# A two-layer decoder step on one core: attention groups regrouped, the last weight chunk cut by tokens, and four waits of the blocks split or reordered

## The reference

```python
for i in range(2):
    x = x + 0.5 * swiglu(rmsnorm(x, ...), w_in, w_out)      # ffn1, inner width 2816
    h = rmsnorm(x, ...)
    y = s5_mixer(h, ...) if i == 0 else hgrn2_mixer(h, ...) # diagonal SSM / gated linear recurrence, 8 heads
    x = x + y
    x = x + cross_attend(rmsnorm(x, ...), mem_k[i], mem_v[i], w_q, w_o)  # 4 heads of 256, 256 memory tokens
    x = x + 0.5 * swiglu(rmsnorm(x, ...), w_in, w_out)      # ffn2
x = rmsnorm(x, final_norm)
```

## Time and profile before

| | us |
|---|---|
| median of 3 runs (lowest, highest) | 2386.51 (2385.75, 2387.01) |
| the profiled execution, its whole time | 2385.19 |
| its span, first to last instruction | 2383.4 |
| PE busy in it | 2351.9 |
| DVE busy | 1291.9 |
| ACT busy | 872.1 |
| POOL busy | 605.3 |

### The profile page before, as it was taken

One profiled execution on the slowest core, in us unless ns is written; L12 is line 12 of the kernel. 1 busy time (PEld: TensorE's weight loads), 2 busy tenths in 40 slices (PEclk: granted clock), 3 DMA queues, 4 the chain that ended last, 5 costly groups with the idle time before them and its releaser, 6 DMA issues.

```text
span 2383.4 us, 50169 instructions
## 1 busy us (share of the span) xinstructions
PE 2351.9 (99%) x21068; PEld 2289.6 (96%) x21068; DVE 1291.9 (54%) x1903; ACT 872.1 (37%) x1398; POOL 605.3 (25%) x591
## 2 busy tenths in 40 slices
PE   8999999999999999999999999999999999999999
PEld 8999999889979999999999999999998969999998
DVE  6654643964575543446543344577777666443442
ACT  4422333543233331232333233267774233221322
POOL 3779957431103000004111010442122103000003
PEclk9999999999999999999999999999999999999999
DMA  5456445563563333333543333333332653333332
GB/s 161 131 156 152 118 122 162 178 177 106 152 237 93 95 95 91 98 103 94 160 116 110 104 104 111 91 99 101 101 108 75 211 186 89 97 93 93 97 101 85
DMA packets 483707, 289.19 MB, mean 121 GB/s; under 512 B 22289, under 2 KB 466962, under 8 KB 482514
## 3 DMA queue, kind: packets, MB, share of 16 engines
q1 hardware_dynamic: 477856, 280.66, 39.8%
q0 software_dynamic: 560, 1.84, 0.6%
q10 hardware_dynamic: 5122, 4.25, 0.5%
HBM read 258.86 MB, written 27.85 MB: 120 GB/s over the span
## 4 chain that ended last, share of the span: by engine, by line
PE 90%; POOL 3%; DVE 3%; ACT 1%; DMA 1%; issue 1%; ACTq 0%; DVEq 0%; SPq 0%; POOLq 0%
PE lin L2918 51%; PE lin L2923 25%; PE mis L2414 3%; PE mis L2553 1%; POOL sTmp L720 1%; PE lin L2501 1%; POOL sGe L721 1%; PE lin L2885 1%; POOL sGe L719 1%; POOL sFe L721 1%; PE mis L2716 0%; PE lin L2666 0%; PE lin L2534 0%; PE mis L2534 0%; DMA raw<-in_xattn_w_kv_dram 0%
## 5 line engine op out<-in xcount | busy, mean ns | idle before, releaser
L1777 DVE TENSOR_TENSOR w_lo<-raw,w_hi 128x1024 fp32r<-128x1024 f32 (+1 forms) x322 | 463.2, 1439 | 300.0 <-ACT w_hi L1307 299.5
L1307 ACT ACTIVATE w_hi<-raw 128x1024 fp32r<-128x1024 f32 (+1 forms) x328 | 364.8, 1112 | 303.8 <-PE lin L2923 247.5
L2918 PE MATMUL lin<-a_rear,w_hi 128*128 128x264 f32 x3552 | 455.7, 279 | 0.0
L2918 PE MATMUL lin<-a_front,w_hi 128*128 128x256 f32 x3552 | 451.6, 279 | 1.1 <-DVE a_rear L1790 0.7
L2918 PEld LDWEIGHTS lin<-a_rear,w_hi 128*128 128x128 f32 x3552 | 432.9, 188 | 0.0
L2918 PEld LDWEIGHTS lin<-a_front,w_hi 128*128 128x128 f32 x3552 | 424.5, 188 | 4.5 <-issue 1.8
L2923 PE MATMUL lin<-a_rear,w_lo 128*128 128x264 f32 x1776 | 245.1, 278 | 0.0
L2923 PE MATMUL lin<-a_front,w_lo 128*128 128x256 f32 x1776 | 240.7, 277 | 2.0 <-DVE w_lo L1777 2.0
L2325 DVE SCALAR_TENSOR_TENSOR xT<-lin,xT 128x520 f32<-128x520 f32 (+1 forms) x88 | 61.6, 700 | 332.4 <-PE lin L2923 331.1
L1040 POOL TENSOR_TENSOR acc<-xT 128x520 f32<-128x520 f32 x8 | 12.2, 1519 | 870.4 <-DVE xT L2325 842.2
L2923 PEld LDWEIGHTS lin<-a_rear,w_lo 128*128 128x128 f32 x1776 | 223.8, 188 | 0.0
(11 more groups left out here) (495 smaller groups left out, 3404.6 us busy)
## 6 DMA issues: line engine op xcount, KB each, us to landing
raw<-in_ffn_w_in_dram SPq DMA_DIRECT2D x176, 512.0 KB, 3.8
raw<-in_ffn_w_out_dram SPq DMA_DIRECT2D x64, 704.0 KB, 4.6
kc<-in_cache_mem_k_dram SPq DMA_DIRECT2D x32, 512.0 KB, 7.1
vc<-in_cache_mem_v_dram SPq DMA_DIRECT2D x16, 1024.0 KB, 8.9
raw<-in_hg_w_in_dram SPq DMA_DIRECT2D x32, 512.0 KB, 4.2
raw<-in_xattn_w_kv_dram SPq DMA_DIRECT2D x16, 512.0 KB, 4.4
raw<-in_s_w_glu_dram SPq DMA_DIRECT2D x16, 512.0 KB, 4.0
raw<-in_xattn_w_q_dram SPq DMA_DIRECT2D x16, 512.0 KB, 4.4
```

The lines of the kernel that those rows point to most:

```text
L1307: act.activation(w_hi[:, j, 0:kt, :], raw[:, j, 0:kt, :], ACT.Copy).then_inc(hi_ready, 1)
L1777: dve.tensor_tensor(low_weights(n, j), raw[:, j, 0:kt, :], w_hi[:, j, 0:kt, :].bitcast(F32), ALU.subtract).then_inc(lo_ready, 1)
L2918: pe.matmul(lpart(j, half), high[:, k, :], (x_lo if u else x_hi)[half][:, k, :], start=start and u == 0 and k == 0, stop=False)
```

## The change

What it does, part by part. (1) In attention the score groups S(0,0) and S(0,1) are done within the query projection, after its chunks 6 and 7; the order of the rest, the banks and the place of the probabilities change; `sample_values` runs for all 8 samples in one go after the last P group (before: six ahead of it, two behind); and ACT instead of DVE empties W. (2) In S5 each FU group waits for its own U group. (3) In HGRN2 T is two transposes of 128 columns. The second chunk of the second projection pair of head 1 has all its high products ahead of the wait for `w_lo`. DVE does `hS` ahead of `values` at h=1, and at h=8 ahead of the reciprocal and of one `h_lo`, which goes behind the samples' states. (4) `projected` finishes chunk 0 ahead of the last two parts of chunk 1, and ACT splits the next weight chunk ahead of `gain_hi` of tile 0. (5) The last weight chunk is done front half first, then rear; between the rear's high and low products PE sums the squares of the first two row tiles and transposes row tile 0.

```diff
-    made = [("B", (b, 0), "dve") for b in range(NS)]
-    XA_EARLY = {4: range(0, 3), 5: range(3, 6), 6: range(6, 8)}
+    made = [("B", (b, 0), "dve") for b in range(NS)] + [("S", (0, 0), "act"), ("S", (0, 1), "act")]
+    XA_EARLY = {4: range(0, 3), 5: range(3, 6), 6: range(6, 9), 7: range(9, 10)}
...
-    made += [("S", (0, 0), "act"), ("S", (0, 1), "act"), ("B", (0, 1), "dve"), ("B", (1, 1), "dve")]
-    made += [("S", (1, 0), "act"), ("B", (2, 1), "dve"), ("P", (0, 0), "act"), ("P", (0, 1), "act")]
-    made += [("S", (1, 1), "act"), ("B", (3, 1), "dve"), ("O", (0, 0), "dve"), ("O", (0, 1), "dve")]
+    made += [("B", (0, 1), "dve"), ("S", (1, 0), "act"), ("B", (1, 1), "dve"), ("P", (0, 0), "act"), ("P", (0, 1), "act")]
+    made += [("S", (1, 1), "act"), ("B", (2, 1), "dve"), ("B", (3, 1), "dve"), ("O", (0, 0), "dve"), ("O", (0, 1), "dve")]
...
-    made += [("S", (3, 0), "act"), ("B", (7, 1), "dve"), ("P", (2, 0), "act"), ("P", (2, 1), "act"), ("T", 0, "act")]
-    made += [("S", (3, 1), "act"), ("O", (2, 0), "dve"), ("W", 0, "dve"), ("O", (2, 1), "dve")]
+    made += [("S", (3, 0), "act"), ("B", (7, 1), "dve"), ("P", (2, 0), "act"), ("P", (2, 1), "act")]
+    made += [("S", (3, 1), "act"), ("T", 0, "act"), ("O", (2, 0), "dve"), ("O", (2, 1), "dve"), ("W", 0, "act")]
...
-                        if u == 2 * MH - 2:
-                            sample_values(layer, range(0, 6))
...
-                            sample_values(layer, range(6, NS))
+                            sample_values(layer, range(NS))
...
                     elif what == "FU":
-                        if a % 8 == 0:
-                            for u in (6, 7):
-                                G.emptied_of(pe, "U", a + u)
+                        G.emptied_of(pe, "U", a)
...
-                        ins = pe.matmul(bank[:, 4 * f:4 * (f + 1)], sRow[:, f, :], ident[:, 0:P:32], start=True, stop=True)
+                        ins = pe.transpose(bank[:, f * P:(f + 1) * P], sRow[:, f, :], ident[:])
...
-                        chunk(p + 1, 1, False)
+                        chunk(p + 1, 1, False, h == 1)
...
-                projected([(1, 5), (0, 6), (1, 6), (0, 7), (1, 7)])
+                projected([(1, 5), (0, 6), (0, 7), (1, 6), (1, 7)])
...
+                    if h == HH:
+                        states(g)
                     if 0 <= e < HH:
                         G.emptied_of(dve, "N", e)
                         dve.reciprocal(rT[:], rT[:]).then_inc(hg["inverse"], 1)
...
+                        if name == "hg_out" and first and j == 0:
+                            split(p + 1, 0, chunk_after(n, 1, last))
                         if after is not None and is_out(name):
                             act.wait_ge(used[j], p + 1)
                             gain_hi(2 * i + j, NORM_ROW[after])
...
+                def last_chunk(p):
+
+                    pe.wait_ge(hi_ready, 2 * p + 2)
+                    wait(pe, used[1], p)
+                    low = low_weights(n, 1)
+                    for half in range(2):
+                        for u, x in enumerate((x_hi, x_lo)):
+                            for k in range(kt):
+                                pe.matmul(lpart(1, half), w_hi[:, 1, k, :], x[half][:, k, :], start=u == 0 and k == 0, stop=False)
+                        if half == 0:
+                            pe.wait_ge(lo_ready, 2 * p + 2)
+                        else:
+                            front_rows()
+                        for k in range(kt):
+                            ins = pe.matmul(lpart(1, half), low[:, k, :], x_hi[half][:, k, :], start=False, stop=k == kt - 1)
+                        ins.then_inc(chunk_done, 1)
...
+            def front_rows():
+
+                pe.wait_ge(root_done, NORMS - 1)
+                pe.wait_ge(y_scale, 1)
+                token_sums(range(0, 2))
+                rows_out(0, range(KD))
...
+            def last_tile(half):
+                cols = COLS[half]
+                dve.wait_ge(chunk_done, 2 * ALL_PAIRS + half)
+                dve.scalar_tensor_tensor(out=xT[:, KD - 1, cols], in0=lpart(1, half), scalar=0.5, in1=xT[:, KD - 1, cols],
+                                         op0=ALU.mult, op1=ALU.add).then_inc(used[1], 1)
+                dve.wait_ge(squares_done, NORMS)
+                dve.wait_ge(y_gained, KD + 2 * half)
+                dve.tensor_tensor(acc[:, cols], acc[:, cols], t2[:, cols], ALU.add).then_inc(y_scale, 1)
```

More of the change, by code:

```diff
@@ L584, in trunk_kernel @@
+    XA_BANKS = [q % 4 for q in range(XA_MAIN)] + [(4, 5, 2, 3, 0, 1)[q % 6] for q in range(len(made) - XA_MAIN)]
     XAG = [Groups(made, xa[l]["fill"], xa[l]["void"], banks=XA_BANKS) for l in range(DEPTH)]
@@ L685, in y_out_of @@
         return dst, bank[0:YC, :].rearrange("n (j t c) -> n t j c", j=4, t=CS)
-    y_order = [(0, 0), (1, 0), (0, 1), (1, 1)] + [(t, half) for t in range(2, 5) for half in range(2)]
+    y_order = [(0, 0), (0, 1), (1, 0), (1, 1), (2, 0), (2, 1), (3, 1), (3, 0), (4, 0), (4, 1)]
+    Y_FRONT, Y_REAR = KD + 1, KD + 3
     def y_bank(t, half):
@@ L1715, in body @@
                             ins.then_inc(h_hi_done, 1)
+                        if name == "xq" and last and j == 1:
+                            attend(layer, range(XA_MAIN - 2, XA_MAIN))
                         if name == "glu" and j == 0:
@@ L1874, in attend @@
                     bank = xa_bank(q)
-                    if (what, a) in WEIGHTED:
-                        weighted(WEIGHTED[what, a])
+                    for u in WEIGHTED.get((what, a), []):
+                        weighted(u)
                     if what == "B":
@@ L2295, in body @@
                             continue
+                        if n == len(ST) - 1 and last and j == 1:
+                            return
                         dve.wait_ge(chunk_done, 2 * p + j + 1)
@@ L2366, in _ @@
                     .then_inc(y_evac["dve"], 1)
+            last_tile(0)
+            dve.wait_ge(root_done, NORMS)
+            dve.reciprocal(rstd[:, 0:2], t1[:, 0:2]).then_inc(y_scale, 1)
+            dve.wait_ge(y_scale, 2)
+            scaled(0)
+            last_tile(1)
+            scaled(1)
+            dve.wait_ge(root_done, NORMS + 1)
+            step.link(dve.reciprocal(rstd[:, 2:4], t1[:, 2:4]))
+            dve.reciprocal(rstd[0:NS, 4:5], t1[0:NS, 4:5]).then_inc(y_scale, 1)
+            dve.wait_ge(y_scale, 4)
+            for t in range(2, 5):
+                scaled(t)
         @block.tensor
@@ L2909, in first_chunks, with chunk @@
                     ins.then_inc(chunk_done, 1)
[L2911 removed]
+                def chunk(p, j, first, low_last=False):
                     pe.wait_ge(hi_ready, 2 * p + j + 1)
@@ L2967, in body @@
                     for j in range(2):
+                        if n == len(ST) - 1 and last and j == 1:
+                            last_chunk(p)
+                            continue
                         if first and r == 0:
@@ L2979, in stream, with rows_out, token_sums @@
                     over_pairs(pe, n, body, hook)
+            def rows_out(t, tiles):
+                cols = P if t < 4 else NS
+                for m in tiles:
+                    pe.wait_ge(y_gained, m + 1 if m < KD - 1 else Y_FRONT if t < 2 else Y_REAR)
+                    ins = pe.transpose(y_bank(t, m // 4)[0:cols, m % 4 * P:(m % 4 + 1) * P],
+                                       yG[:, m, t * P:t * P + cols], ident[:])
+                    if m % 4 == 3:
+                        ins.then_inc(y_tr, 1)
+            def token_sums(tiles):
+                for t in tiles:
+                    cols = slice(t * P, min((t + 1) * P, NT))
+                    ins = pe.matmul(mis[0:cols.stop - cols.start, 0, t:t + 1], acc[:, cols], ones[:, 0:1],
+                                    start=True, stop=True)
+                ins.then_inc(sums_done, 1)
+            def front_rows():
[3 more added lines that the diff above has]
+                rows_out(0, range(KD))
             for n in range(len(ST)):
```

173 lines of the change are left out of this document (90 added, 83 removed).

## The result

The changed kernel takes 2373.50 us (median of 5 runs, 2372.58 to 2375.23) against 2386.51 before (2385.75 to 2387.01). The ratio is 0.9947, interval 0.9933 to 0.9962: faster by 0.53%. Forecast were 2376.4 and a range of 2373.0 to 2381.5, so the sign and the range held and the gain was 2.9 us larger than the sum. 2373.5 lies only 0.5 above the range's lower end. The profiled executions are 2385.19 before and 2372.95 after, spans 2383.4 and 2371.2: 12.2 us, where the sum said 10.15.

The account below looks back on a forecast made before the run. PE was taken as the bound (busy 2351.9 of 2383.4 us) except at the end; 2.2 + 3.1 + 0.3 + 1.6 + 0.25 + 0.7 + 2.0 = 10.15 us less, median 2376.4 us, range 2373 to 2381.5.

Parts of the forecast that it names:

- End: Last weight chunk in two token halves: first output tiles leave earlier, 2.2 us less, bounds 0.8 and 3.0.
- Attention: Two attention layers: first O group starts 0.85 earlier, the 1.2 wait ahead of T goes; 3.1 us for both.
- what is late next: In attention, per layer: W 0.25, and copies ahead of O(2,0) with the last value tile 0.2, taken off the gain.
- The last value tile: Attention's sample_values: sample 7's load lands 6.2 us after the start, just in time after seven samples; priced at 0.1.
- the sign that was to make the prediction wrong: In attention: a wait of PE within sample_values would make the prediction wrong.
- Rival (a): Attention's sample 7 load lands late: 8.9 us gives 2384.0, 14.3 gives 2394.8; chance 0.08, of which 0.03 slower.
- T: HGRN2: two transposes at 0.12 take 0.24 instead of 0.46, eight times; 1.6 us less.
- Rival (b): HGRN2's paired transposes don't overlap: 1.1 us lost instead of 1.6 won, 2379.1; chance 0.07.
- Head 1: HGRN2 h=1: the 1.54 wait for w_lo goes, 0.6 and 0.7 come back; 0.25 us stays, bounds 0 and 1.54.
- h=8: HGRN2: PE's 0.70 wait for hS goes, a reciprocal and an h_lo no longer ahead of it; 0.7 us, bound 0.
- Output projection: HGRN2's output projection: PE's 1.97 wait for ACT's w_hi of the next chunk goes; 2.0 us, bound 1.0.
- S5: FU 8's 0.99 wait goes, but a later wait, read as missing instructions, grows; 0.3 us, bounds 0 and 1.0.

Follow-up runs that it names:

- a_B11_first: Changed kernel with B(1,1) ahead of S(1,0) again, so DVE makes its four products before S(1,0)'s maximum; 2376.76 us in one execution.
- a_T_old: Changed kernel with attention's T ahead of S(3,1) again, W still on ACT and behind O(2,1); 2375.59 us in one execution.
- after_again: The changed kernel measured once more, unaltered, on the same chip as the five-edit version; 2371.69 us, ratio 0.9938.
- b_T: The kernel before with HGRN2's T as two transposes of sRow and nothing else; 2381.22 us in one execution.
- b_hgout: The kernel before with the output projection's edit alone (earlier split of next weights, (0,7) ahead of (1,6)); 2382.99 us, ratio 0.9989.
- a_best: Changed kernel with five small edits to attention's order and loads, head 1's weight split and m_lo's load; 2371.78 us, ratio 0.9946.
- (2) of a_best: One of that version's five edits to the changed kernel: value loads of samples 1 and 2 moved behind sample 4's keys; not timed alone.
- b_end: The kernel before with the new end (last weight chunk in two halves) and nothing else; 2385.24 us in one execution.
- a_mlo_late: Changed kernel with m_lo's 1 MB load waiting for FU group 10 instead of following m_hi at once; 2372.94 us, ratio 0.9942.

## Why the prediction was right, and where it missed

- **End, 2.2 forecast, 2.20 measured** (2.25 alone). The step was right as worked: no stall for `w_lo`, and from the first tile's write the transfers hide PE's rear.
- **Attention, 3.1 forecast, 4.45 measured.** The mechanism held in both halves: a_B11_first gave the first wait back and a_T_old the second. Up to the first O group layer 0 gained 0.91 (0.85 forecast), behind it 1.24 (0.75 forecast). Mis-sized was the term "what is late next", 0.45 a layer for W, O(2,0) and the last value tile. No wait for W or O(2,0) is in the changed kernel's list. And of the first O group's wait 0.41 stayed, not 0.55, while the 0.41 ahead of the second P group, which the sum had left out, went, and 0.34 ahead of B(3,1) came.
- **The last value tile, priced at 0.1.** It landed just in time: PE's 128 records took 7.35 in layer 0 and 7.06 in layer 1, and after_again names the wait, 0.17 for the load. So the sign that was to make the prediction wrong, a wait within `sample_values`, did show, but as small as the sum had it (0.1 to 0.3). Rival (a) had the right place; its landing times of 8.9 us and more don't come where nothing else is in flight (5.2 and 4.9 here).
- **T, 1.6 forecast, 2.05 measured** (b_T: 1.93 for seven, 0.12 for the eighth). Rival (b), transposes that don't overlap, is out. So is a price of two times the 275 ns of the Trainium skill (TensorE: Matmul & The Clock Gate, Part 4: PE-mode transpose): two of them hold the next line up by 0.14 to 0.19.
- **Head 1, 0.25 forecast.** As worked out, the 1.54 came back as 0.78 for `hS` and 0.53 for `w_lo` (0.6 and 0.7 were forecast; its own times, 1603.1 less 1602.4 and 1607.75 less 1607.0, give 0.7 and 0.75, so 0.1 for the term). 0.13 stayed: 0.93 gained from the chunk's first product to `hg_outputs`, less 0.80 behind.
- **h=8, 0.7 forecast, 0.75 measured**, of which 0.12 is T's by b_T.
- **Output projection, 2.0 forecast, 3.64 measured.** This is the step that fell short, on the good side: "PE waits 1.97 for ACT's `w_hi`", and that wait was taken to cost 1.97. The wait was priced rightly: against b_T, where the clock stayed (12.10), the 10.00 are 2.1 less. What the sum left out is the clock behind it, though the trace of before shows it at 0.50, and the earlier trace rows has 2.08 for eight products that take 1.1 elsewhere. b_hgout gets the 3.64 alone.
- **S5, 0.3 forecast.** "I read it as missing instructions" was right. "If they come at a fixed time" was not: their time is set by the loads in front of them. The finer wait brought 0.2 in this pair (0.55 without the clock's 0.35) and about 0.5 in the mean, and in the profiled execution the clock took 1.71 behind it, which by the other profiles was chance.

The clock's two entries cancel in this pair of profiles (+1.7, -1.7), so the 12.2 stay 12.2 without them, against 10.15. That they cancel is luck. What is over is attention (1.35), S5 with the stretch behind it (0.6: 0.20 and -1.00 with the clock's 1.71 given back, against 0.3), T (0.33 in its line) and 0.3 of small things, less 0.52 at the start. The medians lie 13.0 apart, because the profiled execution of before was 1.32 below its median and that of the changed kernel 0.55 below.

## What to carry to other kernels

Read the granted clock behind every idle time of PE near 2 us before pricing it: the products at half speed can cost nearly as much again as the wait, in some executions and not in others, so one profile doesn't give the price. Where a wait stands between two others, name who is queued on the engine that releases it, and count its instructions from one row: that gave 1.36 for one B group, and the chip gave 1.2. When single executions scatter by more than the effect, cut the timeline between the same instructions of both kernels; most stretches repeat to 0.1 us. In a stretch whose DMA engines are full, moving a load can move the wait with it, as (2) of a_best did.

## What the runs showed of the hardware

- Behind PE idle times of 1.97 to 2.27 us the granted clock sometimes fell from 1.00 to 0.50 (2.4 to 1.2 GHz), costing 1.71 each time, and sometimes not, at the same place with the same idle time (1.97 ahead of the output projection: two of three; 2.27: one of two; 1.98 and 1.99 in S5: one of three). Behind the 23 idle times of 1.37 to 1.72 us in the fourteen profiles (the kernel's start and end aside) it never fell. But it also fell at 424 to 425, behind two short waits (0.88 and 0.45), in three of fourteen profiles. That makes part of the scatter of single executions, in steps of 1.7; how large a part, no run shows.
- At the start the first rows of 8 products took 1.9 to 2.1 us in seven of the fourteen profiles and 1.2 in the other seven; the stretch up to S5 was 1.0 longer in the mean of the first seven (415.55 against 414.56). In two of these (b_end, a_mlo_late) the trace's record of the clock begins only behind these rows, and the windows print 1.00 for them. The Trainium skill (TensorE: Matmul & The Clock Gate, Part 1) calls the slow stretch at a kernel's start run-variable; the profiles agree.
- A 16 KB block of PE's instructions comes late behind bulk loads: up to 3.1 us later against the start of FU 8 than with none in flight, and PE goes on 2.2 to 2.5 us after the packet.
